# Attention units of two kinds in alternation, and banded scores over all 128 rows with zeroed keys

## The chip, the cores and the metric

The kernel runs on one core of a Trainium2 chip (trn2). The metric is the device time of one execution in microseconds (us). The core has a matrix engine (TensorE, PE in the rows; PEld is its weight loading), a vector engine (DVE), an activation engine (ACT), GpSimd (POOL) and a sync engine (SP) that issues DMAs; each runs its own instruction stream, and semaphores order them against each other.

## The reference, cut to what matters

Two layers of a backbone over 512 latent tokens and 256 context tokens. Each layer mixes tokens by three groups of heads, then runs a mixture of experts. Only two of the head groups matter here:

```
# banded heads (6 query heads, 2 key/value groups of 3 heads each, head size 64)
s = q @ k.T * 64 ** -0.5          # latent queries: |qpos - kpos| <= 128 among latents, and all 256 context keys
p = softmax(concat([s, sink]))    # one learned sink logit for each head
o = p[..., :-1] @ v
# latent-attention heads (4 heads, 64 + 32 = 96 wide queries and keys, values 64 wide)
s = (qn @ kn.T + qr @ kr.T) * 96 ** -0.5      # latent queries: all 768 keys
o = softmax(s) @ v
# context queries of both kinds see the 256 context keys alone; layer 2 has no context queries
```

Everything is float32.

## The kernel before, in words

The kernel is a row of phases with a barrier between them: in each layer the projections (`phase_front`), the attention of the two head groups above (`phase_attention`), the preparation and scan of the third group, the merge, the routing, the experts and their combination. The change touches `phase_attention` alone. It is called from `mixer` once for each layer, with `nq` = 6 query blocks of 128 in the first layer (4 latent blocks, 2 context blocks) and 4 in the second.

The phase works through units. A unit is one head and one block of 128 queries. The list `units` has the banded heads first (6 heads x nq blocks), then the latent-attention heads (4 x nq): 36 and 24 units in the first layer, 24 and 16 in the second. A banded unit of a latent block has its own key block, its neighbours and the two context blocks: 4 blocks (512 keys) for the first and the last latent block, 5 (640 keys) for the two inner ones. A latent-attention unit of a latent block has all 6 blocks (768 keys). A unit of a context block has 2 blocks (256 keys), whatever its kind.

What a unit does, and where:

- `score` (PE, lines 874 and 875): queries times keys into one of two score buffers in PSUM; line 874 does the latent keys, line 875 the 256 context keys. In a banded unit the contraction is over the 64 rows of the head's key group g: queries of group 0 lie in partitions 0 to 63 of `sqT`, those of group 1 in 64 to 127, and the keys of the groups likewise in `skT`. In a latent-attention unit it is over 96 rows. It waits until the exponentials of the unit two before are done.
- `bias` (DVE): in banded units the band's masks are added to the outer blocks (line 917), then the row maximum (918) and its scaling (923 and 924, or 926).
- `exps` (ACT): the sink's exponential in banded units (964), then the exponentials of the scores with their sum (965).
- `turn` (PE, 881): one transpose for each key block.
- the copy of the transposed blocks to SBUF (ACT, 976).
- `values` (PE, 891): transposed exponentials (weights) times values (64 columns), two instructions for each key block.
- `norm` and `write` (DVE, 932, 933 and 939).

The order on PE is written out: score(u+1), values(u-1), turn(u). On ACT it is the copy of unit u, then the exponentials of unit u+2. On DVE it is bias(u), write(u-2), norm(u-1). At the end SP waits for all units and stores the result (858).

Of the kernel before, what the change touches and what calls it, by code (L numbers as in the profile page):

```python
# [16 lines left out]
P = 128  # L17
# [4 lines left out]
NLT, NT = SEQ // P, (SEQ + CTXN) // P  # L22
NTOK = NT * P
# [3 lines left out]
SWA_H, SWA_KV, HD = 6, 2, 64  # L27
GH = 6
MH, MNOPE, MROPE = 4, 64, 32
# [163 lines left out]
def build(nc, A, out):  # L193
# [12 lines left out]
    with outer:  # L206
        arena = Arena(outer.enter_context(nc.sbuf_tensor("arena", [P, ARENA_WORDS], F32)), ARENA_WORDS)
        sbuf = arena.take
# [613 lines left out]


        def phase_attention(l, nq, vb, sqT, skT, mqT, mkT, mv, cat):
            units = []
            for h in range(SWA_H + MH):
                for i in range(nq):
                    swa = h < SWA_H
                    if i >= NLT:
                        local = []  # L830
                    elif swa:
                        local = list(range(max(i - 1, 0), min(i + 2, NLT)))
                    else:
                        local = list(range(NLT))
                    units.append((h, i, swa, local, local + list(range(NLT, NT))))
            NU = len(units)
            st, S = ExitStack(), Sems(nc, f"at{l}")
            with st:
# [3 lines left out]
                nb = sbuf(st, "nb", [P, 2])  # L842
                es = sbuf(st, "es", [P, 4, 2])
                den = sbuf(st, "den", [P, 4])
                cat_out = S("cat_out")
                step, scored, nb_done, exp_done, turned, et_done, pv_done, out_done = (
                    S("step"), S("scored"), S("nb_done"), S("exp_done"), S("turned"), S("et_done"), S("pv_done"), S("out_done"))
# [4 lines left out]
                with nc.Block() as block:  # L852
                    @block.sync
                    def _(sp):

                        sp.wait_ge(out_done, NU)
                        for a, b in ((0, SWA_H * HD), ((SWA_H + GH) * HD, D)):
                            sp.dma_start(cat_dram[0:nq * P, a:b].rearrange("(i p) n -> p i n", p=P), cat[:, :, a:b]).then_inc(cat_out, 16)
                        sp.wait_ge(cat_out, 32)

                    @block.tensor
                    def _(pe):
                        def score(u):
                            h, i, swa, local, keys = units[u]
                            if u >= 2:
                                pe.wait_ge(exp_done, u - 1)
                            if swa:
                                g, j = h // 3, h % 3
                                q, k = sqT[64 * g:64 * g + 64, j, i * P:(i + 1) * P], skT[64 * g:64 * g + 64, :]
                            else:  # L870
                                q, k = mqT[0:MQ, h - SWA_H, i * P:(i + 1) * P], mkT[0:MQ, h - SWA_H, :]
                            s = sflat(u)
                            if local:
                                nc.tensor.matmul(s[:, span(units[u])[0]:512], q, k[:, local[0] * P:(local[-1] + 1) * P], start=True, stop=True)
                            nc.tensor.matmul(s[:, 512:512 + CTXN], q, k[:, SEQ:NTOK], start=True, stop=True).then_inc(scored, 1)

                        def turn(u):
                            pe.wait_ge(exp_done, u + 1)
                            n = len(units[u][4])
                            for c in range(n):  # L880
                                last = nc.tensor.transpose(tflat[:, c * P:(c + 1) * P], E[:, u % 2, c * P:(c + 1) * P], cst("ident"))
                            last.then_inc(turned, 1)

                        def values(u):
                            h, i, swa, local, keys = units[u]
                            pe.wait_ge(et_done, u + 1)
                            if u >= 2:
                                pe.wait_ge(out_done, u - 1)
                            for c, kt in enumerate(keys):
                                v = vb[:, kt, (h // 3) * HD:(h // 3 + 1) * HD] if swa else mv[:, kt, h - SWA_H, :]  # L890
                                last = nc.tensor.matmul(psum[:, 6 + u % 2, 0:HD], ET[:, u % 2, c * P:(c + 1) * P], v,  # L891
                                                        start=(c == 0), stop=(c == len(keys) - 1))
                            last.then_inc(pv_done, 1)

                        score(0)
                        for u in range(NU):
                            if u + 1 < NU:
                                score(u + 1)
                            if u:
                                values(u - 1)  # L900
                            turn(u)
                        values(NU - 1)

                    @block.vector
                    def _(dve):
# [29 lines left out]
                        def write(u):  # L935
# [4 lines left out]
                                                    ALU.mult).then_inc(out_done, 1)  # L940
                            dve.wait_ge(out_done, u + 1)

                        for u in range(NU):
                            bias(u)
                            if u >= 2:
                                write(u - 2)
                            if u >= 1:
                                norm(u - 1)
# [5 lines left out]
                    @block.scalar  # L954
                    def _(act):
                        def exps(u):
                            h, i, swa, local, keys = units[u]
                            a, b = span(units[u])
                            act.wait_ge(nb_done, u + 1)
                            if u >= 2:  # L960
                                act.wait_ge(turned, u - 1)
                            bias = nb[:, u % 2:u % 2 + 1]
                            if swa:
                                nc.scalar.activation(es[:, u % 4, 1:2], par(l, "sink", h, h + 1), ACT.Exp, bias=bias)
                            nc.scalar.activation(E[:, u % 2, 0:b - a], sflat(u)[:, a:b], ACT.Exp, bias=bias,
                                                 scale=HD ** -0.5 if swa else MQ ** -0.5,
                                                 accum_out=es[:, u % 4, 0:1]).then_inc(exp_done, 1)

                        for u in range(min(2, NU)):
                            exps(u)  # L970
                        for u in range(NU):
                            n = len(units[u][4]) * P
                            act.wait_ge(turned, u + 1)
                            if u >= 2:
                                act.wait_ge(pv_done, u - 1)
                            nc.scalar.copy(ET[:, u % 2, 0:n], tflat[:, 0:n]).then_inc(et_done, 1)  # L976
                            if u + 2 < NU:
                                exps(u + 2)
# [1210 lines left out]
```

## Time and profile before

| | us |
|---|---|
| median of 3 runs | 4321.46 |
| lowest and highest | 4319.16 to 4323.74 |
| the profiled execution | 4320.12 |
| its span (first to last instruction) | 4318.3 |
| mean granted TensorE clock over the span | 0.864 of full speed |
| PE busy | 3515.8 (81%) |
| DVE, ACT, POOL busy | 1138.8, 948.8, 584.1 |
| DMA | 788.23 MB, mean 183 GB/s |

The page divides the span into 40 slices of some 108 us and gives for each the busy tenths of an engine and the granted TensorE clock. The clock has two levels, 2.4 GHz (1.00) and 1.2 GHz (0.50); a value between them is a mean over a stretch that has both. Attention is in the fifth to seventh slice (first layer) and in the 25th to 27th (second layer). A windows view gives busy time and clock of any stretch; a timeline lists instructions in order of time.

### The profile page before, as it was taken

Reading aid. Unit: us, or ns where it says so; the run is one execution under the profiler, and the core shown is the slowest. Engines: PE = TensorE matmul, PEld = TensorE weight load, DVE = VectorE, ACT = ScalarE, POOL = GpSimd, SP = SyncE. Lnnn points to the kernel's source line nnn. Section 1 sums busy time; section 2 is a strip of 40 time slices with the busy share of each in tenths; the row PEclk is TensorE's granted clock in tenths of the full one; section 3 lists DMA queues with packets and bytes.
Section 4 is the critical chain, followed back from the end, with each engine's and each line's share of the span. In section 5 each row is a group of like instructions: output and inputs, shape, how many; then the busy total and the mean of one; then the engine's idle time right before and its main releaser. Section 6 shows DMA issues by size and latency. Waiting matters only on the chain. (4 is left out here: it accounts for less than half of the span.)

```text
span 4318.3 us, 60172 instructions
## 1 busy us (share of the span) xinstructions
PE 3515.8 (81%) x22700; PEld 2039.4 (47%) x22701; DVE 1138.8 (26%) x2446; ACT 948.8 (22%) x1697; POOL 584.1 (14%) x648
## 2 busy tenths in 40 slices
PE   6699896975618999999990598989752899999991
PEld 2355675863314444444440354769631444444440
DVE  0242443442230111111115443334423011111115
ACT  1222332221102222222220222232210222222220
POOL 0010002320040000000004010023203000000003
PEclk8799568997758999999995698589875999999995
DMA  9410006202105888688767310000110689999955
GB/s 418 180 55 8 3 1 238 96 24 99 40 8 222 325 333 341 258 338 313 302 257 284 120 56 6 1 14 4 48 65 18 253 335 359 367 365 359 365 204 224
DMA packets 142744, 788.23 MB, mean 183 GB/s; under 512 B 16560, under 2 KB 36912, under 8 KB 105776
## 3 DMA queue, kind: packets, MB, share of 16 engines
q1 hardware_dynamic: 82976, 577.93, 34.0%
q0 software_dynamic: 37120, 125.89, 8.1%
q10 hardware_dynamic: 22464, 81.80, 4.6%
q8 instruction: 135, 2.21, 0.2%
q14 instruction: 49, 0.40, 0.0%
HBM read 649.09 MB, written 139.62 MB: 183 GB/s over the span
## 5 line engine op out<-in xcount | busy, mean ns | idle before, releaser
L1882 PE MATMUL psum<-arena 128*128 x2496 | 1107.3, 597 | 8.2 <-issue 8.2
L1882 PEld LDWEIGHTS psum<-arena 128*128 128x128 f32 x2496 | 463.5, 191 | 584.7 <-issue 584.7
L1893 PE MATMUL psum<-arena 128*128 x1248 | 550.6, 594 | 0.0
L726 PE MATMUL psum<-arena 128*128 128x480 f32 (+3 forms) x1088 | 400.0, 524 | 2.2 <-ACT arena L580 2.2
L1861 POOL DMA_INDIRECT arena<-h,arena x160 | 150.4, 940 | 1654.2 <-PE psum L1876 1639.7
L1893 PEld LDWEIGHTS psum<-arena 128*128 128x128 f32 x1248 | 230.7, 190 | 261.2 <-issue 261.2
L726 PEld LDWEIGHTS psum<-arena 128*128 128x128 f32 x1088 | 206.5, 193 | 175.8 <-issue 166.2
L1876 PE MATMUL psum<-arena 128*128 128x128 f32 x1280 | 169.6, 276 | 142.8 <-DMA arena<-h,arena 142.8
L1876 PEld LDWEIGHTS psum<-arena 128*128 128x128 f32 x1280 | 149.9, 143 | 185.7 <-DMA arena<-h,arena 144.6
L1951 ACT ACTIVATE arena<-psum 128x256 f32<-128x256 f32 x156 | 60.3, 386 | 780.7 <-PE psum L1882 780.7
L1992 DVE COPY arena<-psum 128x512 f32<-128x512 f32 x156 | 107.9, 692 | 450.7 <-PE psum L1893 450.7
L1936 ACT COPY arena<-psum 128x1024 f32<-128x1024 f32 x160 | 162.0, 1012 | 127.0 <-PE psum L1876 127.0
L354 PE MATMUL psum<-arena 128*128 128x512 f32 x96 | 56.8, 758 | 156.6 <-DVE arena L342 156.6
L1981 DVE TENSOR_TENSOR arena<-arena,psum 128x256 f32<-128x256 f32 x78 | 32.9, 422 | 572.4 <-ACT arena L1951 572.4
L891 PEld LDWEIGHTS psum<-arena 128*128 128x128 f32 x896 | 157.3, 264 | 55.7 <-ACT arena L976 29.5
L1983 DVE COPY arena<-psum 128x256 f32<-128x256 f32 x78 | 33.2, 425 | 555.4 <-PE psum L1888 555.4
L891 PE MATMUL psum<-arena 128*128 128x64 f32 x896 | 170.3, 356 | 9.3 <-ACT arena L976 9.3
L1588 PE MATMUL psum<-arena 128*128 128x512 f32 x320 | 156.8, 653 | 17.1 <-DMA arena<-in_w_out 17.1
L1958 ACT COPY arena<-psum 128x512 f32<-128x512 f32 x156 | 91.4, 586 | 311.3 <-PE psum L1893 311.3
L1951 ACT ACT_TABLE_LOAD x78 | 100.1, 1283 | 216.9 <-issue 216.9
L1570 PE MATMUL psum<-arena 128*128 128x128 f32 x160 | 35.0, 406 | 131.8 <-DVE arena L1623 113.5
L2083 DVE SCALAR_TENSOR_TENSOR arena<-arena 128x1024 f32<-128x1024 f32 x80 | 102.8, 1285 | 44.4 <-DMA arena<-y_slots,arena 41.8
(311 smaller groups left out, 3873.8 us busy)
## 6 DMA issues: line engine op xcount, KB each, us to landing
arena<-in_w_gu SPq DMA_DIRECT2D x130, 2048.0 KB, 8.6
arena<-in_w_dn SPq DMA_DIRECT2D x130, 1024.0 KB, 12.0
y_slots<-arena ACTq DMA_DIRECT2D x156, 512.0 KB
arena<-in_ada SPq DMA_DIRECT2D x24, 2048.0 KB, 17.2
y_slots<-arena SPq DMA_DIRECT2D x8, 4096.0 KB, 34.8
arena<-xres SPq DMA_DIRECT2D x32, 512.0 KB, 5.8
arena<-in_w_gdn SPq DMA_DIRECT2D x6, 1536.0 KB, 13.2
arena<-in_w_out SPq DMA_DIRECT2D x2, 4096.0 KB
```

Source lines behind the costliest of these rows:

```text
L726: last = nc.tensor.matmul(bank(n, wide), lhsT[:, k], rhs[:, k], start=(k == 0), stop=(k == DK - 1))
L891: last = nc.tensor.matmul(psum[:, 6 + u % 2, 0:HD], ET[:, u % 2, c * P:(c + 1) * P], v, start=(c == 0), stop=(c == len(keys) - 1))
L1588: last = nc.tensor.matmul(psum[:, 2 + n, :], cT[:, i % 2, k * P:(k + 1) * P], wo[:, k, n * 512:(n + 1) * 512], start=(k == 0), stop=(k == ...
L1861: nc.gpsimd.indirect_dma_start(xg[:, b % 2], None, h2_dram, bass.IndirectOffsetOnAxis(ap=idx[:, b:b + 1], axis=0)).then_inc(gathered[b % 2 ...
L1876: last = nc.tensor.transpose(psum[:, k // 4, (k % 4) * P:(k % 4 + 1) * P], xg[:, r, k * P:(k + 1) * P], cst("ident"))
L1882: last = nc.tensor.matmul(psum[:, 2 + r, :], xT[:, r, k * P:(k + 1) * P], W[:, bass.ds(slot + k * 2 * DE, 2 * DE)], start=(k == 0), stop=( ...
L1893: last = nc.tensor.matmul(psum[:, (LEFT, RIGHT)[n][r], :], hT[:, r, j * P:(j + 1) * P], W[:, bass.ds(slot + DK * 2 * DE + j * D + n * 512, ...
L1936: nc.scalar.copy(xT[:, r].rearrange("p (b n) -> p b n", b=2), psum[:, 0:2, :]).then_inc(xT_ready, 1)
L1951: nc.scalar.activation(sg[:, r], psum[:, 2 + r, 0:DE], ACT.Silu).then_inc(silu_done, 1)
L1958: nc.scalar.copy(yb[:, r, 0:512], psum[:, LEFT[r], :]).then_inc(ys_ready, 1)
L1992: nc.vector.tensor_copy(yb[:, r, 512:D], psum[:, RIGHT[r], :]).then_inc(yv_ready, 1)
L2083: nc.vector.scalar_tensor_tensor(out=acc[:, i % 2], in0=G[:, n % NG], scalar=wk[:, i, k:k + 1], in1=acc[:, i % 2] if k else sh[:, i % 2], ...
```

## The change

1. The list of units is no longer all banded units and then all latent-attention units: after each banded unit come 0 or 1 latent-attention units, in the pattern banded, banded, latent, banded, latent. Within a kind the order is as before.
2. A new buffer `kz` holds the banded keys once for each key group, over all 128 partitions, with the other group's 64 partitions zeroed. DVE zeroes them (one memset of 64 x 768 for each group), ACT copies the keys (one copy of 64 x 768 for each group) at the start of its stream, and PE waits for all four before its first score.
3. The banded scores contract over all 128 partitions: weights are `sqT` with the queries of both groups, the moving side is `kz` of the head's group. The zeroed rows add nothing to the sum.

```diff
@@ -822,17 +822,22 @@
 
 
         def phase_attention(l, nq, vb, sqT, skT, mqT, mkT, mv, cat):
+            def unit(h, i):
+                swa = h < SWA_H
+                if i >= NLT:
+                    local = []
+                elif swa:
+                    local = list(range(max(i - 1, 0), min(i + 2, NLT)))
+                else:
+                    local = list(range(NLT))
+                return h, i, swa, local, local + list(range(NLT, NT))
+
+            window = [unit(h, i) for h in range(SWA_H) for i in range(nq)]
+            full = [unit(SWA_H + h, i) for h in range(MH) for i in range(nq)]
             units = []
-            for h in range(SWA_H + MH):
-                for i in range(nq):
-                    swa = h < SWA_H
-                    if i >= NLT:
-                        local = []
-                    elif swa:
-                        local = list(range(max(i - 1, 0), min(i + 2, NLT)))
-                    else:
-                        local = list(range(NLT))
-                    units.append((h, i, swa, local, local + list(range(NLT, NT))))
+            for k, un in enumerate(window):
+                units.append(un)
+                units += full[k * len(full) // len(window):(k + 1) * len(full) // len(window)]
             NU = len(units)
             st, S = ExitStack(), Sems(nc, f"at{l}")
             with st:
@@ -842,6 +847,8 @@
                 nb = sbuf(st, "nb", [P, 2])
                 es = sbuf(st, "es", [P, 4, 2])
                 den = sbuf(st, "den", [P, 4])
+                kz = sbuf(st, "kz", [P, SWA_KV, NTOK])
+                kz_ready = S("kz_ready")
                 cat_out = S("cat_out")
                 step, scored, nb_done, exp_done, turned, et_done, pv_done, out_done = (
                     S("step"), S("scored"), S("nb_done"), S("exp_done"), S("turned"), S("et_done"), S("pv_done"), S("out_done"))
@@ -866,7 +873,7 @@
                                 pe.wait_ge(exp_done, u - 1)
                             if swa:
                                 g, j = h // 3, h % 3
-                                q, k = sqT[64 * g:64 * g + 64, j, i * P:(i + 1) * P], skT[64 * g:64 * g + 64, :]
+                                q, k = sqT[:, j, i * P:(i + 1) * P], kz[:, g]
                             else:
                                 q, k = mqT[0:MQ, h - SWA_H, i * P:(i + 1) * P], mkT[0:MQ, h - SWA_H, :]
                             s = sflat(u)
@@ -892,6 +899,7 @@
                                                         start=(c == 0), stop=(c == len(keys) - 1))
                             last.then_inc(pv_done, 1)
 
+                        pe.wait_ge(kz_ready, 2 * SWA_KV)
                         score(0)
                         for u in range(NU):
                             if u + 1 < NU:
@@ -940,6 +948,8 @@
                                                     ALU.mult).then_inc(out_done, 1)
                             dve.wait_ge(out_done, u + 1)
 
+                        for g in range(SWA_KV):
+                            nc.vector.memset(kz[64 - 64 * g:128 - 64 * g, g], 0.0).then_inc(kz_ready, 1)
                         for u in range(NU):
                             bias(u)
                             if u >= 2:
@@ -966,6 +976,8 @@
                                                  scale=HD ** -0.5 if swa else MQ ** -0.5,
                                                  accum_out=es[:, u % 4, 0:1]).then_inc(exp_done, 1)
 
+                        for g in range(SWA_KV):
+                            nc.scalar.copy(kz[64 * g:64 * g + 64, g], skT[64 * g:64 * g + 64, :]).then_inc(kz_ready, 1)
                         for u in range(min(2, NU)):
                             exps(u)
                         for u in range(NU):
```

## Rows read from the trace of the kernel before

**Rows 1.** Part 2 of the page: PE busy tenths and granted clock in 40 slices.
```profile
PE   6699896975618999999990598989752899999991
PEclk8799568997758999999995698589875999999995
```

**Rows 2.** Windows: stretch, then busy us of PE, PEld, DVE, ACT, POOL, clock, DMA.
```profile
456.00:608.00 152.00, 151.58 (x497) 108.71 (x497) 64.90 (x242) 50.22 (x141) 0.00 (x0) 0.50 0.00 1
620.00:676.00 56.00, 50.81 (x335) 39.68 (x334) 25.98 (x77) 27.48 (x57) 0.00 (x0) 1.00 0.00 1
...
608.00:620.00 12.00, 12.00 (x38) 8.40 (x38) 3.93 (x13) 3.60 (x9) 0.00 (x0) 0.52 0.00 0
...
682.00:688.00 6.00, 4.27 (x24) 3.44 (x24) 1.33 (x7) 1.31 (x4) 0.00 (x0) 0.69 0.01 1
```

**Rows 3.** Timeline: first instruction and last write of attention, first layer.
```profile
452.60 1.28 ACT L964 ACT_TABLE_LOAD   x1 [0.92 <-PEq L152]
...
687.30 0.28 DVE L939 TENSOR_SCALAR arena<-psum,arena 128x64 f32<-128x64 f32 x1 [1.52 <-PE psum L891]
```

**Rows 4.** Timeline: the same of the second layer.
```profile
2681.55 1.28 ACT L964 ACT_TABLE_LOAD   x1 [0.92 <-PEq L152]
...
2864.85 0.28 DVE L939 TENSOR_SCALAR arena<-psum,arena 128x64 f32<-128x64 f32 x1 [2.62 <-PE psum L891]
```

**Rows 5.** Timeline, second layer, two banded units: start, us, engine, line, shape, count.
```profile
2742.30 2.40 PE L891 MATMUL psum<-arena 128*128 128x64 f32 x10
2744.49 1.06 PE L881 MATMUL psum<-arena 128*128 128x128 f32 x4
2745.48 1.65 PE L874 MATMUL psum<-arena 64*128 64x384 f32 x2
...
2746.93 1.06 PE L875 MATMUL psum<-arena 64*128 64x256 f32 x2
...
2747.91 1.97 PE L891 MATMUL psum<-arena 128*128 128x64 f32 x8
2748.09 0.64 DVE L917 TENSOR_TENSOR psum<-psum,arena 128x128 f32<-128x128 f32 x2 [2.67 <-PE psum L875]
2748.76 0.82 DVE L918 TENSOR_REDUCE arena<-psum 128x1 f32<-128x640 f32 x1
...
2750.05 0.29 ACT L964 ACTIVATE arena<-arena 128x1 f32<-128x1 f32 x1 [3.88 <-DVE arena L924]
...
2751.02 0.57 ACT L976 COPY arena<-psum 128x512 f32<-128x512 f32 x1
```

**Rows 6.** Timeline, second layer, latent-attention units near the start of that part.
```profile
2808.19 1.06 PE L881 MATMUL psum<-arena 128*128 128x128 f32 x4
...
2809.05 1.91 PE L874 MATMUL psum<-arena 96*128 96x512 f32 x2
...
2810.75 0.63 PE L875 MATMUL psum<-arena 96*128 96x256 f32 x2
```

**Rows 7.** Timeline, second layer, latent-attention units later on.
```profile
2826.22 1.02 PE L874 MATMUL psum<-arena 96*128 96x512 f32 x2
...
2827.08 0.59 PE L875 MATMUL psum<-arena 96*128 96x256 f32 x2
...
2827.78 0.96 DVE L918 TENSOR_REDUCE arena<-psum 128x1 f32<-128x768 f32 x1 [1.54 <-PE psum L875]
...
2829.85 0.79 ACT L976 COPY arena<-psum 128x768 f32<-128x768 f32 x1
...
2830.80 1.45 PE L891 MATMUL psum<-arena 128*128 128x64 f32 x12
...
2832.75 1.02 PE L874 MATMUL psum<-arena 96*128 96x512 f32 x2
```

**Rows 8.** Lines by form, 620 to 676 us: count, busy us, mean ns, idle before.
```profile
L891 PE MATMUL psum<-arena 128*128 128x64 f32 x181 | 23.6, 275 | 5.2 <-ACT arena L976 5.2
```

**Rows 9.** Lines by form, 680 to 2680 us: an ACT pass over 128x768 in SBUF.
```profile
L538 ACT ACTIVATE arena<-arena 128x768 f32<-128x768 f32 x6 | 5.0, 841 | 1.2 <-DVE arena L645 1.2
```

## The prediction, made before the result was known

> **What bounds the kernel now.** I read the page's slices first. PE is busy in nine or ten tenths of most slices, so PE or what feeds it sets the time, and the clock row shows where PE is slow: the fifth and sixth slice and the 26th lie at 0.5 to 0.6 although PE is busy for eight or nine tenths [rows 1]. These are the attention phases. Next the windows: while banded units run, PE is busy for 151.58 of 152.00 us, and the granted clock is 0.50, the lower of its two levels (1.2 GHz), from end to end; in the latent-attention units of the same phase it is 1.00 (2.4 GHz) with PE busy for 50.81 of 56.00 us [rows 2]. The second layer shows the same: its banded part has the low clock, and it rises within the first latent-attention units (the last matmul pair of the row group takes 0.63 us where such pairs took 1.06 before) [rows 5, 6]. DMA is idle there (share 0.00) and POOL too. So in the banded part PE alone is the limit, at half its speed, and it is not for want of work.
>
> The stretch at stake is the whole phase: 452.60 to 687.58 us, 235.0 us [rows 3], and 2681.55 to 2865.13 us, 183.6 us [rows 4]; together 418.6 us of the span of 4318.3. The profiled execution took 4320.12 us, 1.8 more than its span and 1.3 less than the median of 4321.46; I sum against the span and carry the difference over to the median.
>
> **What differs between the stretch at half clock and that at full clock.** Not the busy share. A banded unit at the low clock (4 and 5 blocks of keys in turn) has values, transposes and two score matmuls: the values of 5 blocks run from 2742.30 to 2744.49 and transposes of 4 blocks to 2745.48, both over 128 rows; the scores run to 2747.91 over 64 rows [rows 5]. So 2.43 of 5.61 us of PE's time, 43%, goes over 64 rows. A latent-attention unit at the low clock has scores over 96 rows [rows 6] for about 40% of its time, and that is where the clock rose, in both layers. The rest of a unit is the same instructions. That leaves the rows (64 against 96) as the likeliest cause, with the width (384 and 256 columns against 512) second. With keys zeroed over 128 rows the banded unit has more rows in use than the latent-attention unit that raised the clock, and every second or third unit is a latent-attention unit anyway. I take it that the clock rises soon after the first units and stays up.
>
> The Trainium skill (TensorE: Matmul & The Clock Gate, "What's actually happening") says that the clock is set by how busy PE has been recently. By that alone the banded part, which is busy throughout, would have the full clock already, and neither a change of rows nor of order would change it. The trace disagrees with that reading (0.50 beside 151.58 of 152.00 us busy) [rows 2]; by that rule the change would be worth its other parts only, which is the second rival.
>
> **The change part by part.**
>
> *Rows 64 to 128.* At one clock a matmul's time goes by its columns: 512 columns over 96 rows took 1.70 us at the low clock (2809.05 to 2810.75) [rows 6], 3.3 ns a column, and 0.86 us at the full one [rows 7]. The banded matmuls of 64 rows cost more than that: 384 columns took 1.45 us (2745.48 to 2746.93) where 1.28 follow, and 256 columns 0.98 us before the values started, where 0.85 follow; the four transposes ahead took 0.99 us where the same four take 0.86 ahead of a 96-row score [rows 5, 6]. So a banded unit loses 0.17 + 0.13 + 0.14 = 0.44 us beside the 64-row matmuls, and this goes. The Trainium skill (TensorEngine Tiling (Array Packing), "Key Properties") says that changing the tiling mode drains the engine; the 0.14 and 0.13 us at the two borders agree, and nothing in the sum hangs on it.
>
> *Full clock: what a banded unit then takes.* PE's own work per block of keys is 0.43 + 0.43 + 0.21 = 1.07 us at the low clock (score, two values instructions, one transpose) and 0.54 at the full one: 2.7 us for 5 blocks. But PE no longer ends last. Two score buffers make two loops, one for even and one for odd units: score, bias on DVE, exponentials on ACT, copy of the unit before on ACT, its values, the transposes, then the next score of the same buffer. In latent-attention units this loop takes 2832.75 - 2826.22 = 6.53 us for two units, 3.27 each, and PE's own work is 6 x 0.54 = 3.24, so the two are level [rows 7]. For a banded unit of 5 blocks at full clock: score 1.07 and 0.27 until DVE starts (2827.08 + 0.43 to 2827.78) [rows 7]; bias 2748.09 to 2750.05, 1.96; ACT to the copy's start 0.97; the copy 0.57 + 0.11 for the fifth block = 0.68 [rows 5]; 0.16 until the values start [rows 7]; values 1.08; transposes 0.54. Sum 6.73, so 3.37 us a unit. A block less takes from the loop 0.21 (score), 0.14 (reduce, 0.96 against 0.82), some 0.12 (exponentials), 0.11 (copy), 0.21 and 0.11 (PE), 0.90 in all or 0.45 a unit, and a mask less 0.32 or 0.16 a unit [rows 5, 7]. So 4 blocks and one mask take 2.76, a context unit (2 blocks, no mask) 1.70, and a context unit of latent attention 3.27 - 4 x 0.45 = 1.47.
>
> *Order.* Short and long units stand beside each other, and then the two loops and PE don't fit as well. The nearest row is the latent-attention part of the first layer, 4 wide and 2 context units in turn: 181 values instructions in 56 us at 56 for each six units make 17.3 us, with PE waiting for the copy [rows 8], where 4 x 3.27 + 2 x 1.47 = 16.0 is the sum: 8% more. The second layer has no context units; in it units of 4, 5 and 6 blocks alternate, and I take 3% (bounds 0 and 8%). For the first layer I take 7% (bounds 3 and 10%).
>
> *kz.* ACT copies 64 x 768 twice ahead of its first exponential; a pass over 768 columns in SBUF took 0.84 us [rows 9], so 1.6 us in each layer before PE's first score. DVE's two memsets run beside them (the rows have none; DVE's reduce over 768 columns, 0.96 us [rows 7], is the bound that I take for one), covered as long as they take less than the copies, else 0.3 us more. The table load of 1.28 us that now heads ACT's stream [rows 3] goes behind the copies and beside the first score; if it comes ahead of them it adds 1.3 a layer. The wait stands at the head of PE's stream with everything of the phase behind it. Lower bound of all this 0.8, upper 3.0 us a layer.
>
> *Head and tail.* Until the clock rises I allow some 8 us at the low level, as the first layer took most of 12 us from its first latent-attention scores [rows 2]; two units at 5.3 instead of some 3.2 lose 3 us. The last unit has nothing behind it: some 5 us in the first layer and 6 in the second beyond its own period (score, bias, exponentials, transposes, copy and values one after the other).
>
> *Sum.* First layer: 12 x (3.37 + 2.76 + 1.70) = 94.0 and 16 x 3.27 + 8 x 1.47 = 64.1, together 158.1; with 7% 169.2; with 1.6 + 3 + 5 it is 178.8, against 235.0: saved 56.2. Second layer: 12 x (3.37 + 2.76) = 73.6 and 16 x 3.27 = 52.3, together 125.9; with 3% 129.7; with 1.6 + 3 + 6 it is 140.3, against 183.6: saved 43.3. Together 99.5, so a span of 4219 and a time of 4222 us. Barriers stand on both sides of the phase and its stores begin after its last unit, so I let nothing give the gain back or add to it. The bounds of the terms (order, kz, head) move it by -14 and +14 us; short falls of the clock beside context units, as at 682 to 688 us, where it was 0.69 [rows 2], can add 20 more in the first layer.
>
> **The rivals.**
>
> *The clock stays low for the whole phase, with latent attention diluted (slower).* If what counts is something that banded units lack whatever their rows (wide matmuls, or zeros that don't count), the alternation takes away the unbroken run of latent-attention units in which the clock now rises. PE then sets the time at 1.07 us a block: first layer 132 banded and 112 latent blocks, 260 us; second 108 and 96, 218 us; with 8 us of head and tail each 494, against 418.6: 75 slower, 4397. It decides when latent units, some half of the blocks, no longer raise the clock. For it speaks that nothing in the trace shows a banded unit at full clock; against, that in the second layer it rose between latent scores while the last banded unit still ran among them (the four transposes of 2808.19 are a banded unit's, a latent one has six) [rows 6]. Chance 0.06.
>
> *The rows make no difference and the clock goes up and down with the mix.* Half the time at each level gives (319 + 494) / 2 = 407, 12 faster, 4310; a third at the low level 4280. Beside it stands the busy rule of the skill named above. For it: the level is held by something not seen; against: the low level held without a flicker for 152 us of banded units and the high one for 56 us of latent-attention units [rows 2]. Chance 0.09 for 4262 to 4330.
>
> *The change raises the clock, but DVE or the order bounds the units more than I sum.* DVE's work in a banded unit of 5 blocks is 1.96 us [rows 5], 0.28 for the write [rows 4] and two one-column operations that I put at 0.4, 2.6 us, under the 3.37 of the loop. If the mixed loops cost 15% instead of 7 and 3, it is 28 us more: 4250. It lies in the range.
>
> **How the numbers follow.** Forecast (clock up for most of the phase, 4200 to 4262): 0.84; partly up: 0.09; all low: 0.06; something outside the phase: 0.01. The predicted time is the sum's, 4222. The range 4200 to 4262 takes in the terms' bounds and the falls beside context units. A difference under 0.2% (9 us) can't be told from none here: faster 0.91, same 0.02 (of the mix case), slower 0.07.
>
> **What would show it.** In the profile after: a granted clock of 1.00 through both attention phases save the first 10 us; transposes and 256-column score pairs of banded units at some 0.27 and 0.6 us as in rows 7; a span of each phase of 179 and 140 us; PE busy for some 80 to 85% of it and the first idle time of PE before the values, waiting for ACT's copy. A clock of 0.50 there refutes the step from rows to clock. A right clock with phases above 190 and 150 us would show the loop or the order mis-sized.

## The result

The changed kernel takes 4219.57 us (median of 4 runs, 4215.80 to 4225.03) against 4320.31 us for the kernel before in the same comparison: a ratio of 0.9766, 95% interval 0.9752 to 0.9781. The forecast was 4222 us. The profiled execution has a span of 4218.4 us; that of before had 4318.3.

The page of the changed kernel, PE's busy tenths and its granted clock in 40 slices (each slice is now some 105 us):

```profile
PE   6699777956519999999990598979661999999991
...
PEclk8799898987659999999995699999775999999995
```

The fifth and sixth slices show 8 and 9 where [rows 1] have 5 and 6, and the 26th 9 instead of 5. PE is busy for less of them (7 and 7 tenths instead of 8 and 9): at twice the clock it waits. The windows of the two attention phases, from the first copy of ACT to the last write of DVE (busy us of PE, PEld, DVE, ACT, POOL, then clock, DMA share, GB/s):

```profile
449.50:627.40 177.90, 149.62 (x932) 117.95 (x932) 101.26 (x350) 87.89 (x219) 0.00 (x0) 0.95 0.00 1
2627.60:2765.90 138.30, 121.14 (x772) 96.15 (x772) 77.00 (x246) 68.11 (x147) 0.00 (x0) 0.97 0.00 1
```

The phases took 235.0 and 183.6 us before [rows 3, 4], so 57.1 and 45.3 us are gone, 102.4 together. The rest of the span went from 3899.7 to 3902.2 us; in the runs below it lies between 3896 and 3906, so that is play between executions. A phase here, and in all runs below, is counted from ACT's first instruction to DVE's last write in the one execution that was profiled; the medians are of all executions.

The start of the first phase, ACT, DVE and PE (timeline: start, us, engine, line, operation, count, idle before and its releaser):

```profile
449.51 1.68 ACT L980 COPY arena<-arena 64x768 f32<-64x768 f32 x2 [0.93 <-PEq L152]
449.72 0.70 DVE L952 MEMSET arena<- 64x768 f32 x1 [4.24 <-PEq L152]
450.63 0.70 DVE L952 MEMSET arena<- 64x768 f32 x1 [0.22 <-issue]
451.21 1.28 ACT L974 ACT_TABLE_LOAD   x1
451.39 1.22 PE L881 MATMUL psum<-arena 128*128 128x256 f32 x2 [3.91 <-DVE arena L952]
...
454.54 1.06 PE L882 MATMUL psum<-arena 128*128 128x256 f32 x2
...
456.01 0.66 PE L888 MATMUL psum<-arena 128*128 128x128 f32 x4 [0.41 <-ACT arena L975]
```

PE's first score comes 1.88 us after ACT's first instruction, and the table load stands behind the copies. Four transposes take 0.66 us at 456.01 where they took 1.06 at the low clock [rows 5]: the clock has risen 4.6 us after the first score, before the first score of a latent-attention unit (456.50 us).

But the clock isn't held throughout, and PE now waits for ACT's copy. First PE's waits from 460 to 620 us (us in total, times, longest; L898 is the values matmul, L988 the copy), then PE alone around the first fall:

```profile
PE psum L898 <- ACT arena L988: 22.7, 32, 1.7
```

```profile
493.11 0.60 PE L882 MATMUL psum<-arena 96*128 96x256 f32 x2
495.44 0.66 PE L898 MATMUL psum<-arena 128*128 128x64 f32 x4 [1.73 <-ACT arena L988]
495.93 0.72 PE L888 MATMUL psum<-arena 128*128 128x128 f32 x5
496.49 0.76 PE L881 MATMUL psum<-arena 128*128 128x256 f32 x2
497.04 1.06 PE L882 MATMUL psum<-arena 128*128 128x256 f32 x2
497.89 2.23 PE L898 MATMUL psum<-arena 128*128 128x64 f32 x10
```

A 2-block unit waits 1.73 us for the copy behind a wide unit's exponentials, and a moment later the matmuls are at the low clock (10 values instructions in 2.23 us instead of the 1.22 at 491.82 us), until 504. There are two more such falls, each of some 3 to 4 us, at 582 us, after a wait of 1.74 us, and, in the second layer, at 2733 us, after a wait of 1.29 us. The two longest waits of the first phase stand right before its two falls, but the same wait of 1.29 us at 2667 us was followed by none: that the waits bring the falls about isn't shown.

### The profile page after: what moved, and what is told of

It reads as the page before. It is cut to its first block and busy times, and to the rows that moved or that the text cites. A ratio compares the mean times of both kernels' runs of the same rounds, so it can differ in the third digit from the quotient of the medians.

```text
span 4218.4 us, 60180 instructions
## 1 busy us (share of the span) xinstructions
PE 3383.0 (80%) x22700; PEld 1952.3 (46%) x22701; DVE 1140.6 (27%) x2450; ACT 950.6 (23%) x1701; POOL 584.6 (14%) x648
## 5 line engine op out<-in xcount | busy, mean ns | idle before, releaser
L1894 PEld LDWEIGHTS psum<-arena 128*128 128x128 f32 x2496 | 463.4, 191 | 584.8 <-issue 584.8
L1905 PEld LDWEIGHTS psum<-arena 128*128 128x128 f32 x1248 | 230.7, 190 | 261.2 <-issue 261.2
L726 PEld LDWEIGHTS psum<-arena 128*128 128x128 f32 x1088 | 206.1, 193 | 175.1 <-issue 165.5
L1888 PEld LDWEIGHTS psum<-arena 128*128 128x128 f32 x1280 | 150.0, 143 | 185.8 <-DMA arena<-h,arena 144.6
L898 PE MATMUL psum<-arena 128*128 128x64 f32 x896 | 120.4, 280 | 40.1 <-ACT arena L988 39.9
L898 PEld LDWEIGHTS psum<-arena 128*128 128x128 f32 x896 | 111.7, 194 | 69.6 <-ACT arena L988 67.5
```

What stands on the lines that cost most here:

```text
L726: last = nc.tensor.matmul(bank(n, wide), lhsT[:, k], rhs[:, k], start=(k == 0), stop=(k == DK - 1))
L1888: last = nc.tensor.transpose(psum[:, k // 4, (k % 4) * P:(k % 4 + 1) * P], xg[:, r, k * P:(k + 1) * P], cst("ident"))
L1894: last = nc.tensor.matmul(psum[:, 2 + r, :], xT[:, r, k * P:(k + 1) * P], W[:, bass.ds(slot + k * 2 * DE, 2 * DE)], start=(k == 0), stop=( ...
L1905: last = nc.tensor.matmul(psum[:, (LEFT, RIGHT)[n][r], :], hT[:, r, j * P:(j + 1) * P], W[:, bass.ds(slot + DK * 2 * DE + j * D + n * 512, ...
```

## The experiments

Runs with one execution are marked as such: the kernel before, timed beside them, lay anywhere from 4314 to 4327 us, and a difference of less than that is not read from them.

Two theories stood against each other for the clock. The first: what counts is how many of the array's rows a matmul uses; 64 are too few. The second: the mix with latent-attention units (their order, or their 512-column matmuls) does it. Then for what bounds a unit at full clock: the loop through DVE and ACT, or PE's own work, and what the order costs.

### The order alone

In `score`, banded units again take `sqT` and `skT` over their own 64 rows, and kz is gone:

```diff
-                                q, k = sqT[:, j, i * P:(i + 1) * P], kz[:, g]
+                                q, k = sqT[64 * g:64 * g + 64, j, i * P:(i + 1) * P], skT[64 * g:64 * g + 64, :]
```

> The alternated order alone: banded scores over 64 rows as before, no kz. Theory (the rows in use decide the clock): banded units of 64 rows pull the clock down and latent-attention units of 96 rows pull it up, so it goes up and down with the mix, granted mean between 0.5 and 0.9 over the two phases, and the phases take 340 to 480 us together (before 418.6, after 314.7): 4240 to 4385 us. Rival A (the order alone raises the clock): 1.00 nearly throughout, and only the 64-row loss of 0.44 us a banded unit at the low clock, at most half of it at the full one, 13 us, comes on top: about 4233 us. Rival B (64-row units hold it down wholly): 0.50 throughout, about 4405 us.

Measured: 4286.57 us, ratio 0.9921 (0.9905 to 0.9938). The profiled execution was the shortest of four (4272.75 us; the others took 4285.40 to 4293.20); in it the phases take 217.8 and 157.0 us, 374.8 together, at a mean clock of 0.74 and 0.83. The windows of this kernel:

```profile
470.00:490.00 20.00, 18.12 (x116) 13.89 (x115) 11.02 (x39) 9.82 (x25) 0.00 (x0) 1.00 0.00 1
550.00:570.00 20.00, 19.21 (x66) 14.52 (x66) 8.28 (x27) 7.31 (x17) 0.00 (x0) 0.55 0.01 1
570.00:590.00 20.00, 20.00 (x71) 15.44 (x71) 6.77 (x25) 6.10 (x16) 0.00 (x0) 0.50 0.00 0
```

The clock goes up and comes down with the same pattern of units running, and once stays down for 75 us (552 to 627). By the medians, the order alone takes 35 us off, where the whole change takes 101.

### The rows alone

```diff
-            units = []
-            for k, un in enumerate(window):
-                units.append(un)
-                units += full[k * len(full) // len(window):(k + 1) * len(full) // len(window)]
+            units = window + full
```

> kz and the scores over 128 rows alone, in the order of before (all banded units, then all latent-attention units). Theory (rows decide): the clock is 1.00 in the banded units within some 8 us and stays, apart from short falls beside pairs of context units; the two phases take 305 to 320 us together, 4212 to 4225 us, the same as the whole change within 0.2%. Rival (the mix with latent-attention units is what raises it): 0.50 through the banded part, which then costs 1.07 us a block, 141 and 115 us instead of 156 and 122, about 4300 us.

Measured: 4208.39 us, ratio 0.9732 (0.9716 to 0.9748), so 11 us less than the whole change and less than the 4212 to 4225 expected; the two intervals of the ratios don't meet. The phases take 173.3 and 133.4 us, 306.7 together. Windows of this kernel:

```profile
460.00:620.00 160.00, 136.44 (x898) 107.78 (x898) 94.99 (x330) 81.23 (x207) 0.00 (x0) 1.00 0.00 1
2630.00:2745.00 115.00, 106.66 (x707) 85.08 (x704) 69.08 (x222) 58.43 (x132) 0.00 (x0) 1.00 0.00 1
```

With banded units alone for the first 100 us the clock is 1.00 without a fall, though PE is busy for 136 of 160 us, less than the 151.58 of 152.00 of [rows 2] at 0.50. So widening the scores from 64 to 128 rows is the cause and the alternation isn't needed for it. With the rows wide it costs; with 64 rows it gave 35 us, so the two halves don't add up.

Where it costs can be read from the two profiles. In the first layer PE waits for ACT's copy as long in both (25.1 us in the whole change, 25.5 here, both from 450 to 626 us), for in the plain order too pairs of short context units stand beside long ones. But PE's matmuls take 149.62 us there and 145.12 here: 4.5 us more, and the phase is 4.6 us longer. That is the price of the two falls, 10 us at the low clock. In the second layer the whole change has 2.2 us more of matmuls and 3.4 us more of waits (14.3 against 10.9), in a phase that is 4.9 us longer.

### Latent attention over 64 rows

```diff
-                                q, k = mqT[0:MQ, h - SWA_H, i * P:(i + 1) * P], mkT[0:MQ, h - SWA_H, :]
+                                q, k = mqT[0:64, h - SWA_H, i * P:(i + 1) * P], mkT[0:64, h - SWA_H, :]
```

> The kernel of before with the latent-attention scores over the first 64 of their 96 rows (the other 32 rows of the contraction are left out, so part of the scores is missing; the instructions and columns are the same). Theory (rows decide): the clock no longer rises in the latent-attention part and stays 0.50 through both phases; that part takes 112 + 96 blocks at 1.07 us, 222 us and some 10 us of 64-row loss, instead of 135: about 4410 us. Rival (the width of 512 columns, or the share of other instructions, raises it): as before, 1.00 from about 10 us into that part, 4320 us.

Measured, in one execution: 4434.61 us; the phases take 291.4 and 239.8 us at a clock of 0.50 from end to end. A window in the latent-attention part of the first layer:

```profile
620.00:740.00 120.00, 119.54 (x392) 85.03 (x393) 29.45 (x88) 32.67 (x66) 0.00 (x0) 0.50 0.00 1
```

The same columns, widths and order, with 64 rows instead of 96, and the rise that the kernel before shows at 620 us [rows 2] doesn't come. It came out 25 us above the expected 4410. A part of them is seen: in steady state a wide unit takes 6.89 us (exponentials at 2880.00 and 2886.89), 0.47 more than 6 x 1.07, which over 32 wide units is 15 us where 10 were allowed for the loss of 64 rows. The rest stays open.

### Narrower matmuls in latent attention

```diff
-                            if local:
+                            if local and not swa:
+                                for c in range(2):
+                                    nc.tensor.matmul(s[:, 256 * c:256 * c + 256], q, k[:, 256 * c:256 * c + 256], start=True, stop=True)
+                            elif local:
```

> The kernel of before with the 512-column score matmul of the latent-attention units cut into two of 256 columns, 96 rows as they are. Theory (rows decide): the clock rises in that part as before and the time is 4320 us, up to 8 us more for the added weight loads. Rival (matmuls of 512 columns raise it): 0.50 through both phases, about 4400 us.

Measured, in one execution: 4324.48 us. The clock rises as before:

```profile
470.00:600.00 130.00, 130.00 (x426) 93.25 (x426) 55.49 (x208) 42.02 (x120) 0.00 (x0) 0.50 0.00 1
620.00:680.00 60.00, 54.21 (x386) 47.47 (x384) 27.34 (x82) 29.53 (x63) 0.00 (x0) 1.00 0.00 1
```

The width of 512 columns isn't needed for the rise.

### 96 rows for three heads, then 64

The order is that of before; kz has zeroes in 32 more rows than group 0 needs.

```diff
-                                q, k = sqT[:, j, i * P:(i + 1) * P], kz[:, g]
+                                q, k = (sqT[0:96, j, i * P:(i + 1) * P], kz[0:96, 0]) if g == 0 else (
+                                    sqT[64:128, j, i * P:(i + 1) * P], skT[64:128, :])
```

> In the order of before, heads 0 to 2 score over 96 rows (the keys of group 0 with 32 zeroed rows), heads 3 to 5 over their own 64 rows, latent attention over 96. Theory (rows in use decide, and 96 are enough whatever the width): the clock is 1.00 in the first half of the banded part, falls to 0.50 within some 10 us of the fourth head, and rises again in latent attention: about 50 us saved of 4321, 4272 us. Rival (banded units need more than 96 rows because their matmuls are narrower): 0.50 through the whole banded part, about 4316 us (less of the 64-row loss).

Measured, in one execution: 4243.75 us, 28 less than expected. Windows of the first layer: 96 rows until 511 us, 64 rows until 567, then latent attention:

```profile
454.00:480.00 26.00, 25.45 (x87) 20.47 (x88) 11.73 (x42) 9.49 (x24) 0.00 (x0) 0.50 0.00 0
484.00:511.00 27.00, 21.48 (x147) 17.31 (x146) 18.17 (x69) 14.72 (x42) 0.00 (x0) 1.00 0.01 2
511.00:548.00 37.00, 32.28 (x188) 22.91 (x186) 25.44 (x96) 18.38 (x55) 0.00 (x0) 1.00 0.00 1
550.00:567.00 17.00, 16.50 (x63) 12.97 (x62) 6.67 (x26) 6.49 (x18) 0.00 (x0) 0.52 0.00 1
```

96 rows raise the clock too, but only some 28 us after the first score, and 18 us in the second layer, where 128 rows took 3 to 8 us in the eight kernels here whose first head has them. And with the clock up, 64-row units kept it for 40 us, from 511 to 551, and for 21 in the second layer. So the theory needs a second half: few rows don't raise the clock, but they don't drop it at once. The next run asks that.

One rival no run separates from the number of rows: the losses at the borders between 64-row and other matmuls that the prediction measured at the low clock. They are there at the full clock too, as PE's rows of the second layer of this run show (four transposes take 0.45 us ahead of a 96-row score and 0.53 ahead of a 64-row one):

```profile
2660.93 0.61 PE L886 MATMUL psum<-arena 128*128 128x128 f32 x4
2661.38 0.81 PE L879 MATMUL psum<-arena 96*128 96x384 f32 x2
...
2685.50 0.61 PE L886 MATMUL psum<-arena 128*128 128x128 f32 x4
2686.03 0.91 PE L879 MATMUL psum<-arena 64*128 64x384 f32 x2
```

Against them as the whole cause speaks that 96 rows have no such loss and yet raised the clock so much later than 128.

### One head over 128 rows, the rest over 64

```diff
-                                q, k = sqT[:, j, i * P:(i + 1) * P], kz[:, g]
+                                q, k = (sqT[:, j, i * P:(i + 1) * P], kz[:, 0]) if h == 0 else (
+                                    sqT[64 * g:64 * g + 64, j, i * P:(i + 1) * P], skT[64 * g:64 * g + 64, :])
```

> In the order of before, head 0 alone scores over 128 rows, heads 1 to 5 over their own 64, latent attention over 96. It asks whether the rows are needed to raise the clock only or also to hold it. Theory 1 (64-row units can't raise it, and hold it only for a time, as the 40 us in e5): 1.00 within 10 us of the start, a fall to 0.50 some 20 to 60 us after head 0 that stays until latent attention: 45 to 60 us saved in the two phases of before, about 4270 us. Theory 2 (once high, it stays whatever the rows): the phases take as long as in e2, 307 us, and up to 13 more, about 4215 us. Theory 3 (falls at once): 0.50 from the second head on, 4300 us.

Measured, in one execution: 4271.70 us. The 64-row units begin at 471 us in the first layer and at 2658 in the second:

```profile
471.00:521.00 50.00, 43.83 (x261) 31.80 (x261) 34.13 (x129) 25.17 (x75) 0.00 (x0) 1.00 0.00 1
530.00:568.00 38.00, 38.00 (x128) 27.39 (x126) 14.90 (x57) 12.23 (x34) 0.00 (x0) 0.50 0.00 1
...
2670.00:2750.00 80.00, 80.00 (x265) 58.88 (x264) 31.88 (x112) 23.90 (x60) 0.00 (x0) 0.50 0.00 1
2760.00:2810.00 50.00, 49.99 (x337) 40.04 (x337) 24.48 (x64) 25.05 (x46) 0.00 (x0) 1.00 0.01 1
```

The first theory of the expectation holds in the main: the high clock outlasts the 128-row head by 56 us in one layer (to 527 us) and by 9 us in the other (to 2667 us), where 20 to 60 had been expected, and once it has fallen it stays at 0.50 until latent attention. Why the two layers differ so much is open. So the 0.50 of the kernel before is the level at which both of its phases start, and out of which 64-row units don't bring it.

### The short bias

In banded units one DVE operation instead of two between the maximum and the exponentials, in the kernel with the rows alone:

```diff
-                                ch(nc.vector.tensor_scalar(m, m, HD ** -0.5, par(l, "sink", h, h + 1), ALU.mult, ALU.max))
-                                nc.vector.tensor_scalar(o, m, -1.0, None, ALU.mult).then_inc(nb_done, 1)
+                                nc.vector.tensor_scalar(o, m, -(HD ** -0.5), ns[:, h:h + 1], ALU.mult, ALU.min).then_inc(nb_done, 1)
```

> e2 with one DVE operation less between the row maximum and the exponentials of a banded unit (minimum with the negated sink in one step instead of maximum and then negation). PE's work is the same. Theory (at full clock the loop through DVE and ACT bounds a banded unit, not PE): the operation is 0.15 us and its gap 0.1, half of it a unit, 60 units: 7 us less than e2, of it 4 in the first layer's phase and 3 in the second's. Rival (PE's own work bounds): no difference of the phases' spans beyond 1 us.

Measured: the phases take 171.3 and 131.2 us, 302.5 instead of 306.7: 4.2 us less where the loop theory asked for 7 and the PE theory for 0. The whole time is 4209.29 us, no different from 4208.39: its span outside the phases happened to be 3905.8 against 3900.1 us. These are spans of one execution each, and the medians can't show it. But the second phase, which has the same code and order in the rows alone and in two runs below, took 133.4 us in all three, and 131.2 us both here and in the next run. So 2.2 us there is more than play, and the loop through DVE bounds a part of the units.

### The early start

PE waits first for group 0's keys alone, and ACT copies group 1's after its first two exponentials, on top of the short bias:

```diff
-                        for g in range(SWA_KV):
-                            nc.scalar.copy(kz[64 * g:64 * g + 64, g], skT[64 * g:64 * g + 64, :]).then_inc(kz_ready, 1)
+                        nc.scalar.copy(kz[0:64, 0], skT[0:64, :]).then_inc(kz_ready[0], 1)
                         for u in range(min(2, NU)):
                             exps(u)
+                        nc.scalar.copy(kz[64:128, 1], skT[64:128, :]).then_inc(kz_ready[1], 1)
```

> e6, and PE waits at first for the keys of group 0 alone; group 1's are copied after the first two exponentials and awaited by head 3. Theory: the second copy's 0.84 us leaves the path in each layer, 1.7 us less than e6. Rival (the table load or DVE's memset is late instead): nothing.

Measured: 4211.88 us; the phases take 173.3 and 131.2 us, 304.5 together with a clock of 0.96 and 0.98. PE's first score does come sooner, 0.96 us after ACT's first instruction instead of 1.88, but the 1.7 us are not to be seen: the second layer took the same time, the first 2 us more at a lower mean clock (0.98 before). There the clock rose at 459.8 us and fell again at 463.2 for 3.4 us, right behind the early start. No gain shown.

### Context units set apart

In the kernel with the rows alone, the first layer's blocks go in the order 0, 4, 1, 2, 5, 3:

```diff
-            window = [unit(h, i) for h in range(SWA_H) for i in range(nq)]
-            full = [unit(SWA_H + h, i) for h in range(MH) for i in range(nq)]
+            order = [0, 4, 1, 2, 5, 3] if nq == NT else list(range(nq))
+            window = [unit(h, i) for h in range(SWA_H) for i in order]
+            full = [unit(SWA_H + h, i) for h in range(MH) for i in order]
```

> e2 with the two context units of each head in the first layer set apart (block order 0, 4, 1, 2, 5, 3 instead of 0, 1, 2, 3, 4, 5), so that each stands between wide units, as the alternation of the whole change does more often. The second layer is as in e2. Theory (short units next to long ones make PE wait for ACT's copy, and the clock may fall after such waits): the first layer's phase is 5 to 12 us longer than e2's 173.3, with waits of over 1 us before the values of 2-block units. Rival (only the sum of the units counts): 173 us, and what e2 gains on the whole change comes from somewhere else.

Measured: 4238.88 us, ratio 0.9820 (0.9798 to 0.9842), 30 us more than the rows alone. The first phase takes 200.1 us instead of 173.3; the second is the same (133.4). Windows of the banded part with its head and the first units of latent attention (from 557 us), and of the rest of latent attention:

```profile
456.00:566.00 110.00, 84.14 (x542) 66.87 (x542) 69.22 (x259) 52.09 (x150) 0.00 (x0) 0.97 0.00 1
566.00:646.00 80.00, 70.52 (x371) 56.25 (x370) 28.72 (x86) 30.94 (x66) 0.00 (x0) 0.81 0.00 1
```

Short next to long costs far more than the 5 to 12 us that I had put. Against the rows alone, PE's matmuls take 161.63 us instead of 145.12 in this phase, 16.5 more, with the clock low for 46 of the 200 us, and its waits for the copy 34.4 instead of 25.5. From its rise at 461.5 us the clock holds through the 128-row part, with PE busy for 72 of 95 us (462 to 557); the 96-row part loses it four times (at 571, 605, 615 and 646 us).

### Context units together

The opposite: all wide banded units, the context units of both kinds, then the wide latent-attention units:

```diff
-            units = window + full
+            wide = lambda us: [un for un in us if un[1] < NLT]
+            short = lambda us: [un for un in us if un[1] >= NLT]
+            units = wide(window) + short(window) + short(full) + wide(full)
```

> e2 with the context units of the first layer in one row between the wide banded and the wide latent-attention units, so that short units stand next to long ones at two places only. The second layer is as in e2. Theory (short next to long is what costs beyond the sum of the units): the first layer's phase takes 158 us of units and 11 us of head and tail, 169, against 173.3 in e2: 4204 us. Rival (20 short units in a row use PE too little, the clock falls there): those 20 take some 2.1 us each instead of 1.6, 178 us, 4213 us.

Measured: 4203.55 us, ratio 0.9723 (0.9707 to 0.9740), the lowest median of all; its interval overlaps that of the rows alone, and it is the phases that tell the two apart. The first takes 166.1 us, 7.2 less than with the rows alone, the second 133.4 again. Over the first phase PE waits for the copy for 17.5 us instead of 25.5, and its matmuls take 145.14 us against 145.12. The clock never falls, as it didn't with the rows alone, so the gain is in the waits:

```profile
452.72:618.79 166.07, 145.14 (x932) 112.79 (x932) 102.21 (x350) 85.76 (x219) 0.00 (x0) 0.98 0.00 1
460.00:615.00 155.00, 137.64 (x901) 107.43 (x900) 97.64 (x339) 81.06 (x212) 0.00 (x0) 1.00 0.00 1
```

### Together, with the short bias and the early start

The same order of units in the kernel of the early start:

```diff
-            units = window + full
+            wide = lambda us: [un for un in us if un[1] < NLT]
+            short = lambda us: [un for un in us if un[1] >= NLT]
+            units = wide(window) + short(window) + short(full) + wide(full)
```

> e10 with the shorter bias of e6 and the early start of e7. Theory: the phases take what e10's take less the 4.2 us that e6 took off e2's, 298 to 300 us together, about 4200 us. Rival (what e6 took off was the play between two runs): the same as e10 within 1 us of the two phases.

Measured: 4206.17 us (4197.08 to 4213.10); the phases take 165.0 and 133.3 us, 298.3 against 299.5. The clock's mean in them is 0.97 and 0.96 (0.98 and 0.98 without). In both phases the clock falls again within 7 us of its rise, for 3.4 us at 461 us and for 6.8 us at 2625 us. With the early start this happened in three of four phases (here and in the run of that name), without it in none of the twelve phases whose first head has 128 rows. So the early start may be what loses the gain; the medians can't tell the two kernels apart.

## Why the prediction was right, and where it wasn't

- **What bounds the kernel, and rows as the cause.** Right, and shown but for the border losses that go with 64 rows: the rows alone raise the clock (0.50 to 1.00 in banded units), 64 rows in latent attention keep it from rising, and 512-column matmuls aren't needed for the rise. The Trainium skill (TensorE: Matmul & The Clock Gate, "What's actually happening") has the clock follow how busy PE has been. Taken as the share of time, that doesn't describe this stretch: 0.50 beside 119.54 of 120.00 us busy with 64 rows, 1.00 beside 136.44 of 160.00 us with 128.
- **A banded unit at full clock, 3.37 and 2.76 us.** Right. In the kernel with the rows alone the pairs of 384-column scores of a head's second block follow each other after 12.24 us (2660.40, 2672.64, 2684.89; the rows are below; a head has four units), 3.06 a unit; (3.37 + 2.76) / 2 = 3.07. PE's own work would be 4.5 x 0.54 = 2.4.
- **The sums.** 179 and 140 us were forecast, 177.9 and 138.3 came. That it is so close is in part luck: the 3 us for the head came to nothing in each layer, and the order cost 0.7 and 1.1 us more than its terms of 11.1 and 3.8. PE was busy for 84% and 88% of the phases, where 80 to 85% stood among the signs.
- **Order.** I put 7% and 3%. Against the kernel with context units together the whole change takes 11.8 us longer in the first layer, 7.5% of 158, and 4.9 in the second, 3.9% of 126. The size was right, but what it is made of was not what the prediction had in mind, loops that don't fit: 4.5 of the 11.8 us and some 2 of the 4.9 are slower matmuls, in the falls of the clock. And the expectation for the rows alone took it for a term that the plain order has too. In the first layer it has, from its context units (173.3 us measured, 158.1 + 1.9 + 5 = 165.0 by the units); in the second it has none (1.9 + 73.6 + 52.3 + 6 = 133.8 against 133.4 measured).
- **The alternation as help.** Wrong in the step where I counted the latent-attention units between the banded ones as one more reason for the clock to rise. It rose before the first of them had run a score, and the rows alone are 11 us faster.
- **kz.** 1.88 us to the first score against 1.6 forecast; the copies are 1.68 us for both, the memsets 0.70 each, the second of which ends 0.1 us after the copies and is what PE waits for last.
- **Head.** I gave 8 us at the low clock and 3 us of loss; it was 4.6 us and no loss that can be seen in the second layer's sum.
- **Falls beside context units.** Forecast as up to 20 us more in the first layer; there were two, 10 us at the low clock together, and they cost 4.5 us. The sign that the clock would be 1.00 through both phases save the first 10 us was so not quite met. One fall came in the second layer, which has no context units, and that I had not expected.
- **The rivals.** None came. The clock that goes up and down with the mix is what the order without the rows does (4286.57 us); the rows remove it but for the three short falls. The third, an order that costs 15%, stayed at 7.5 and 3.9%.

The rows for the second point, PE in the kernel with the rows alone:

```profile
2660.40 0.81 PE L878 MATMUL psum<-arena 128*128 128x384 f32 x2
...
2672.64 0.81 PE L878 MATMUL psum<-arena 128*128 128x384 f32 x2
...
2684.89 0.81 PE L878 MATMUL psum<-arena 128*128 128x384 f32 x2
```

## What to carry to other kernels

Where PE is busy all the time and the granted clock is still 0.50, look at how many rows its matmuls contract over: filling the contraction to 128 with zeroes cost nothing in columns here and doubled the clock of all the banded units but the first. Undo each half of such a change by itself: here one half brought more than all of the gain and the other took some back. At full clock, a pipeline of two buffers wants units of like length next to each other; where short and long stood side by side, the engine waited, and now and then lost its clock besides.

## What the runs showed of the hardware that I had not expected

The clock has a memory. 64-row units never raised it in 150 us, yet after other units had raised it they held it for 40 and 21 us in one run and for 56 and 9 us in another. How fast it rises goes with the rows: 3 to 8 us after the first score with 128 rows, 28 and 18 us with 96 in banded units. In the run with the context units apart it held in the 128-row part with PE busy for 72 of 95 us; in the 96-row part behind, with waits of up to 1.5 us, it fell four times. What exactly is weighed, and why the 64-row units held it so differently in two layers, stays open.
